# The gate's modulation columns: row pairs of the weight, four column quarters on separate array columns, the last pair at the 13th tile

## The chip, the cores and the metric

The kernel runs on one core of one Trainium2 chip. The metric is the time of one execution on the device, in microseconds (us). Before the change three runs took 1488.47, 1492.28 and 1495.5 us; the median is 1492.28 us.

## The reference, cut to what matters

One layer of a decoder trunk is computed for a prompt of 2048 rows and for 8 sample rows. Everything starts with a modulation made from a condition vector c, of which there are nine (one for the prompt, eight for the samples):

```python
mod = jnp.einsum("nd,de->ne", jax.nn.silu(c), w_ada) + b_ada      # d = 1024, e = 3 * 1024
shift, scale, gate = jnp.split(mod[:, None, :], 3, axis=-1)
h = _rmsnorm(x, norm_g) * (1.0 + scale) + shift
z = jnp.einsum("nld,de->nle", h, w_in)                             # 3840 columns: 30 tiles of 128
...                                                                # four branches, from z
return x + gate * jnp.einsum("nle,ed->nld", y, w_out)
```

shift and scale are needed ahead of everything else, because h needs them. gate, the last 1024 columns of `mod`, is needed only at the end, when the output projection is scaled by it. The change is about how these 1024 gate columns are computed: nine rows, a sum over 1024, weights of 4 MB.

## The kernel before, in words

Each engine has its own instruction queue, written out by hand, and the queues meet by semaphores. The first stage normalizes x and turns it, and multiplies the shift and scale columns (`mod_chunk`, L899). Then h is split into a high and a low part (`h_hi`, `h_lo`).

The second stage is the input projection: 30 tiles of 128 output columns. `project` (L968) multiplies one tile over five groups of up to 416 rows (banks 0 to 4 of PSUM), for each group 8 steps of the sum by three matmuls (`three`, L934: high by high, high by low, low by high). Meanwhile ScalarE and VectorE split the weights of the next tile (`split_w`) and empty the banks (`evac`), SyncE stores the tile (`store`), and GpSimd's queue loads the weights of the tile after next (`load`). All four follow the same order of tiles (`walk`, L374), numbered t from 0, so that tile 12 is the 13th.

The gate columns stand between tile 1 and tile 2 of this stage. Their weight is cut by columns: four quarters of 256 columns, each with all 8 steps of the sum, 1 MB each, in two buffers `gate_w` (L166). SyncE loads quarters 0 and 1 ahead of the projection (L640 to L644), when the first stage has left the places of the buffers (the squares' scratch `junk` and the modulation's bias `b_mod`). TensorE multiplies a quarter in `gate_columns` (L939): 8 matmuls of 9 by 256 columns into partitions 0 to 8 of bank 5. VectorE adds the bias of the quarter into `mod_gate` (L1533 to L1537) and so frees bank 5 for the next quarter. SyncE loads quarters 2 and 3 into the two buffers as soon as quarters 0 and 1 are multiplied (L684 to L688); in its queue this stands behind the store of tile 1.

From tile 12 on, eight chunks of the pooling and convolution branch run beside the projection. Their rows are loaded back by GpSimd's queue (`chunk_load`, L827) into places that lie over the gate weights' buffers, VectorE works on them (`chunk`, L1447), and TensorE multiplies two small matrices in bank 5 (`pool_matmul`, L949), from tile 13 on, behind the third group of rows.

`mod_gate` is read for the first time at the start of the output stage (L1134). The attention in between (from about 806 us to 1226 us) works on units of 128 queries; its `weigh_values` (L1054) is of interest for one thing: it writes head 0 to partitions 0 to 63 and head 1 to partitions 64 to 127 of the same bank, from matmuls of 64 output columns each (L1067). `decode` has matmuls of 48 columns at partition 0 (L1109) and of 32 columns at partition 64 (L1112).

Of the kernel before, what the change touches and what calls it, by code (L numbers as in the profile page):

```python
# [19 lines left out]
P = 128  # L20
D = 1024
KD = D // P
T = 2048
NS = 8
# [51 lines left out]
def build_program(nc, x_prompt, x_sample, c_t, w_ada, b_ada, norm_g, w_tiles, const, pool_w, pool_scale,  # L76
# [4 lines left out]
    with ExitStack() as ctx:  # L81
# [16 lines left out]
        def sem(name):  # L98
            return ctx.enter_context(nc.semaphore(name))
# [20 lines left out]
        mod_gate = keep.put("mod_gate", [NS + 1, D])  # L120
# [4 lines left out]
        c_silu = keep.put("c_silu", [P, KD, NS + 1])  # L125
# [10 lines left out]
        b_gate = keep.put("b_gate", [NS + 1, D])  # L136
# [6 lines left out]
        slot_at = w_at + 6 * D * 4  # L143
        SLOT = TT * 4
# [18 lines left out]
        junk = Plan(slot_at + 2 * SLOT).put("junk", [P, D])  # L163
        b_mod = Plan(slot_at + 3 * SLOT).put("b_mod", [NS + 1, 2 * D])
        mod_sb = Plan(slot_at + 4 * SLOT).put("mod_sb", [NS + 1, 2 * D])
        gate_w = [Plan(slot_at + (2 + b) * SLOT).put(f"gate_w{b}", [P, KD, 256]) for b in range(2)]  # L166

        cp = Plan(slot_at + 2 * SLOT)
        u_in = cp.put("u_in", [P, 2, HALO + CH])
# [82 lines left out]
        psum = ctx.enter_context(nc.psum_tensor("psum", [P, 8, 512], F32))  # L252
# [4 lines left out]
        x_loaded = [sem(f"x_loaded{i}") for i in range(4)]  # L257
        xs_loaded = sem("xs_loaded")
        ada_loaded = sem("ada_loaded")
        gate_loaded = [sem(f"gate_loaded{i}") for i in range(2)]  # L260
        c_ready = sem("c_ready")
        sumsq = sem("sumsq")
        rstd_ready = sem("rstd_ready")
# [7 lines left out]
        mod_t = sem("mod_t")  # L271
# [12 lines left out]
        gate_mm = sem("gate_mm")  # L284
        gate_added = sem("gate_added")
# [318 lines left out]
        wv = w_ada.rearrange("(k p) e -> p k e", p=P)  # L604
# [6 lines left out]
        def _(sp):  # L611
# [28 lines left out]
            sp.wait_ge(sumsq, 17)  # L640
            sp.wait_ge(mod_added, 4)
            sp.wait_ge(mod_mm, 4)
            for q in range(2):
                sp.dma_start(gate_w[q][:], wv[:, :, 2 * D + 256 * q:2 * D + 256 * q + 256]).then_inc(gate_loaded[q], 16)  # L644

            def nat_store(n, g, t):

# [14 lines left out]
            def store(t, half, ts, kind):  # L662
                b = ts % 2
                one = lambda a, i: a[bass.ds(i, 1), :, :].rearrange("a p t -> p (a t)")
                for n, g in turns(ts - 1) if ts >= 12 else ():
                    nat_store(n, g, ts - 1)
                sp.wait_ge(bank_free[4], t + 1)
                if V0 <= ts < K0:
                    pass
                elif kind == "plain":  # L670
                    sp.dma_start(one(plain_dram, t), main[b][:, 0:T]).then_inc(main_stored[b], 16)
                elif kind == "gate":
                    sp.dma_start(one(gate_dram, t - GATE0), main[b][:, 0:T]).then_inc(main_stored[b], 16)
                else:
                    sp.dma_start(qk_dram[t - K0, 0].rearrange("h r t -> (h r) t"), main_hi[b][:, 0:T].bitcast(F32)).then_inc(
                        main_stored[b], 16)
                    sp.dma_start(qk_dram[t - K0, 1].rearrange("h r t -> (h r) t"), main_lo[b][:, 0:T].bitcast(F32)).then_inc(
                        lo_stored[b], 16)
                if 0 <= ts - CHUNK0 < NCH:
                    n = ts - CHUNK0  # L680
                    sp.wait_ge(yac_ready, n + 1)
                    sp.dma_start(yac_dram[:, :, CH * n:CH * n + CH].rearrange("m p t -> p m t"), yac[:]).then_inc(
                        yac_stored, 16)
                if ts == 1:  # L684
                    for q in range(2):
                        sp.wait_ge(gate_mm, q + 1)
                        sp.dma_start(gate_w[q][:], wv[:, :, 2 * D + 512 + 256 * q:2 * D + 768 + 256 * q]).then_inc(
                            gate_loaded[q], 16)  # L688

            walk(sp, store)  # L690

# [116 lines left out]
        def _(pool):  # L808
# [18 lines left out]
            def chunk_load(n):  # L827
                c0 = CH * n
                if n == 0:
                    for b in range(2):  # L830
                        pool.wait_ge(main_stored[b], 16 * 6)
                else:
                    pool.wait_ge(yac_ready, n)
                h = HALO if n else 0
                h2 = 2 if n else 0
                def rows(a, c, left, dst):
                    pool.dma_start(dst, a[:, :, c - left:c + CH].rearrange("m p t -> p m t")).then_inc(chunk_loaded, 16)
                rows(plain_dram[0:2], c0, h, u_in[:, :, HALO - h:])
                rows(plain_dram[2:4], c0, h2, ch_in[:, :, 2 - h2:])
                rows(plain_dram[4:6], c0, h2, cc_in[:, :, 2 - h2:])  # L840
                rows(plain_dram[6:8], c0, 0, cb_in[:])
                rows(gate_dram[0:4], c0, 0, gate_in[:])
# [45 lines left out]
        def _(pe):  # L888
# [34 lines left out]
            for k in range(KD):  # L923
                m = pe.transpose(psum[:, 0, NS * k:NS * k + NS], x_in[0][0:NS, k * P:(k + 1) * P], ident[0:NS, 0:NS])
# [11 lines left out]
                pe.matmul(out, hi, mlo, start=False, stop=False)  # L936
                return pe.matmul(out, lo, mhi, start=False, stop=stop)  # L937

            def gate_columns(q):  # L939
                b = q % 2  # L940
                pe.wait_ge(gate_loaded[b], 16 * (q // 2 + 1))
                if q:
                    pe.wait_ge(gate_added, q)
                for k in range(KD):
                    m = pe.matmul(psum[0:NS + 1, 5, 0:256], c_silu[:, k, :], gate_w[b][:, k, :],
                                  start=(k == 0), stop=(k == KD - 1))
                m.then_inc(gate_mm, 1)

            def pool_matmul(n):  # L949
                pe.wait_ge(diff_ready, n + 1)  # L950
                for m in range(2):
                    mm = pe.matmul(psum[:, 5, CH * m:CH * m + CH], pool_w_sb[:, m, :], diff[:, m, :],
                                   start=True, stop=True)
                mm.then_inc(pool_mm, 1)
# [35 lines left out]

            project(0, 0, 0)
            project(1, 1, 1)
            for q in range(4):
                gate_columns(q)
            with pe.Fori(1, 6) as i:
                for b in range(2):
                    project(2 * i + b, b, 2)
            project(12, 0, 12)
            with pe.Fori(0, 2) as i:
                for b in range(2):  # L1000
# [132 lines left out]
            for n in range(2):  # L1133
                m = pe.matmul(bank(n), consts[0:NS + 1, C_SELP:C_SELP + P], mod_gate[:, 512 * n:512 * n + 512],  # L1134
                              start=True, stop=True)
# [242 lines left out]
        def _(dve):  # L1378
# [68 lines left out]
            def chunk(n):  # L1447
# [45 lines left out]
                                                    gate_in[:, m, :], ALU.mult, ALU.mult)  # L1493
                last.then_inc(yac_ready, 1)

            def evac(t, half, ts, kind):
                b = ts % 2
                if ts + 1 < NT:
                    split_w((t + 1, ts + 1))
                if kind == "plain" and ts >= 12:  # L1500
                    main_free(dve, ts)
                elif kind == "plain" and ts >= 2:
                    dve.wait_ge(main_stored[b], 16 * half)
                if ts == K0:
                    dve.wait_ge(yac_stored, 16 * NCH)
                if ts >= K0 + 2:
                    dve.wait_ge(lo_stored[b], 16 * ((ts - K0) // 2))
                if K0 < ts < Q0:
                    dve.wait_ge(kv_t, turns(ts - 1)[-1][0] + 1)
                for g, (c0, c1) in enumerate(GROUPS):  # L1510
                    n = min(c1, T) - c0
                    if kind == "plain":
                        dve.wait_ge(group_done, 5 * t + g + 1)
                        last = dve.tensor_copy(main[b][:, c0:c0 + n], bank(g, n))  # L1514
                    elif kind == "gate":
                        if g < 4:
                            continue
                        dve.wait_ge(act_evac, t - GATE0 + 1)
                    else:
                        dve.wait_ge(act_evac, V0 - GATE0 + 5 * (ts - K0) + g + 1)  # L1520
                        last = dve.scalar_tensor_tensor(main_lo[b][:, c0:c0 + n], bank(g, n),  # L1521
                                                        -0.125 if kind == "q" else 1.0,
                                                        main_hi[b][:, c0:c0 + n].bitcast(F32), ALU.mult, ALU.subtract)
                        if kind == "k":
                            last = dve.tensor_copy(k_nat[:, c0:c0 + n], bank(g, n))
                    if g == 4:
                        dve.tensor_copy(zs_t[:, bass.ds(t, 1), :].rearrange("p a s -> p (a s)"),
                                        psum[:, g, n:n + NS]).then_inc(bank_free[g], 1)
                    else:
                        last.then_inc(bank_free[g], 1)  # L1530
                if 0 <= ts - CHUNK0 < NCH:
                    chunk(ts - CHUNK0)
                if ts == 1:  # L1533
                    for q in range(4):
                        dve.wait_ge(gate_mm, q + 1)
                        dve.tensor_tensor(mod_gate[:, 256 * q:256 * q + 256], psum[0:NS + 1, 5, 0:256],
                                          b_gate[:, 256 * q:256 * q + 256], ALU.add).then_inc(gate_added, 1)  # L1537

            walk(dve, evac)

# [412 lines left out]
```

## Time and profile before

| | |
|---|---|
| three runs | 1488.47, 1492.28, 1495.5 us |
| the profiled execution | 1488.72 us, its span from first to last instruction 1485.9 us |
| TensorE busy | 1369.2 us, 92% of the span |
| VectorE busy | 715.7 us, 48% |
| ScalarE busy | 463.3 us, 31% |
| GpSimd busy | 155.0 us, 10% |
| mean granted TensorE clock | 0.971 of full |

All times of a trace are us from the start of the span. The 2.8 us between the span and the time of the profiled execution lie outside the first and last instruction. A matmul on data of type fp32 leaves two records, each with a weight load of its own; one on fp32r leaves one. A record's duration runs from its start to the end of its result, so that records that follow closely overlap, and what one costs in a stream is the distance from start to start.

### The profile page before, as it was taken

The page shows a single profiled execution, that of the slowest core. Times are in us where ns is not written, and L with a number is a line of the kernel's source. Part 1 is how long each engine was busy: PE and PEld are TensorE (multiplying, and loading weights), DVE is VectorE, ACT ScalarE, POOL GpSimd, SP SyncE. Part 2 cuts the span into 40 slices and gives each one's busy share as a digit, 9 for nine tenths or more (in the row PEclk, how much of TensorE's full clock was granted, in tenths as well). Part 3 has the DMA queues.
Part 4 walks back from the last instruction along what each step waited for, and adds up shares of the span by engine and source line. Part 5 has one row for each costly group of instructions (what it writes and reads, how often), then busy time and mean ns, then how long its engine had stood idle before and what let it go on. Part 6 is the DMA issues. An engine that isn't in the chain of part 4 may idle for free.

```text
span 1485.9 us, 21646 instructions
## 1 busy us (share of the span) xinstructions
PE 1369.2 (92%) x7749; PEld 1189.7 (80%) x7749; DVE 715.7 (48%) x1835; ACT 463.3 (31%) x1190; POOL 155.0 (10%) x170
## 2 busy tenths in 40 slices
PE   5789999999999999999997799799979997999996
PEld 2376999999999998999996687678767765877774
DVE  3591111100344544232212557675777646788784
ACT  5530000121111101221111455565558541433431
POOL 0060000000122110000000012101110000111111
PEclk9989999999999999999999799989989998999998
DMA  9613121221353434434314995982594255454531
GB/s 322 225 54 110 57 85 42 85 85 42 114 199 119 152 114 142 136 107 172 116 69 143 234 231 139 250 175 62 127 234 137 94 171 177 154 177 159 172 124 47
DMA packets 125661, 206.31 MB, mean 139 GB/s; under 512 B 12835, under 2 KB 88260, under 8 KB 120045
## 3 DMA queue, kind: packets, MB, share of 16 engines
q1 hardware_dynamic: 112358, 160.12, 36.5%
q0 software_dynamic: 13216, 45.09, 9.3%
q8 instruction: 47, 0.77, 0.2%
q14 instruction: 40, 0.33, 0.1%
HBM read 136.34 MB, written 68.97 MB: 138 GB/s over the span
## 4 chain that ended last, share of the span: by engine, by line
PE 67%; issue 14%; DVE 5%; DMA 5%; SPq 4%; ACT 2%; POOL 2%; DVEq 0%; POOLq 0%; ACTq 0%
PE psum L935 15%; PE psum L936 15%; PE psum L937 15%; PE psum L1040 5%; PE psum L1067 4%; PE psum L1041 3%; PE psum L1051 3%; DMA v_dil<-dil_v_p 2%; SPq L423 2%; PE psum L906 2%; DMA dil_v_p<-kv_nat 2%; PE psum L1076 1%; POOL resid L882 1%; DVE h_f L1441 1%; PE psum L1109 1%
## 5 line engine op out<-in xcount | busy, mean ns | idle before, releaser
L935 PE MATMUL psum<-h_hi,w_hi 128*128 128x416 f32 (+1 forms) x1200 | 423.1, 353 | 12.6 <-POOL h_lo L814 12.6
L936 PE MATMUL psum<-h_lo,w_hi 128*128 128x416 f32 (+1 forms) x1200 | 420.9, 351 | 0.0
L937 PE MATMUL psum<-h_hi,w_lo 128*128 128x416 f32 (+1 forms) x1200 | 419.6, 350 | 0.0
L935 PEld LDWEIGHTS psum<-h_hi,w_hi 128*128 128x128 f32 x1200 | 226.6, 189 | 17.4 <-issue 14.6
L936 PEld LDWEIGHTS psum<-h_lo,w_hi 128*128 128x128 f32 x1200 | 226.8, 189 | 1.5
L937 PEld LDWEIGHTS psum<-h_hi,w_lo 128*128 128x128 f32 x1200 | 226.5, 189 | 1.3
L1308 ACT ACTIVATE probs<-logits,stats 128x256 f32<-128x256 f32 (+1 forms) x352 | 162.2, 462 | 166.9 <-DVE stats L1700 164.6
L1040 PE MATMUL psum<-k_both,q_both 128*128 128x256 f32 x352 | 149.0, 432 | 34.6 <-DMA v_dil<-dil_v_p 22.9
L1700 DVE CUSTOM_DVE_ANT_0 logits<-psum,bias_dil 128x256 f32<-128x256 f32 (+1 forms) x288 | 94.3, 363 | 98.9 <-PE psum L1041 78.6
L1040 PEld LDWEIGHTS psum<-k_both,q_both 128*128 128x128 f32 x352 | 93.6, 266 | 57.9 <-issue 31.9
L935 PE MATMUL psum<-wo_hi,y_hi 128*128 128x512 f32 x288 | 116.8, 405 | 10.9 <-DVE y_lo L1770 10.5
L1041 PE MATMUL psum<-k_both,q_both 128*128 128x256 f32 x352 | 124.0, 361 | 0.0
L936 PE MATMUL psum<-wo_lo,y_hi 128*128 128x512 f32 x288 | 113.7, 395 | 0.0
L937 PE MATMUL psum<-wo_hi,y_lo 128*128 128x512 f32 x288 | 113.7, 395 | 0.0
L1521 DVE SCALAR_TENSOR_TENSOR main_lo<-psum,main_hi 128x416 fp32r<-128x416 f32 (+1 forms) x45 | 26.3, 584 | 164.5 <-ACT main_hi L1270 164.5
L1514 DVE COPY main<-psum 128x416 f32<-128x416 f32 (+1 forms) x60 | 34.2, 583 | 143.5 <-PE psum L937 143.5
L1051 PE MATMUL psum<-consts,probs 128*128 128x128 f32 x574 | 96.7, 282 | 3.4 <-DVE probs_t L1688 3.4
L1222 ACT CAST w_hi<-w_raw 128x1024 fp32r<-128x1024 f32 x30 | 31.3, 1042 | 211.2 <-PE psum L937 189.1
L1041 PEld LDWEIGHTS psum<-k_both,q_both 128*128 128x128 f32 x352 | 96.0, 273 | 0.0
L1686 DVE COPY probs_t<-psum 128x512 f32<-128x512 f32 x111 | 76.7, 691 | 23.8 <-PE psum L1067 23.2
L1067 PE MATMUL psum<-probs_t,v_dil 128*64 128x128 f32 x900 | 82.3, 291 | 0.0
L1051 PEld LDWEIGHTS psum<-consts,probs 128*128 128x128 f32 x574 | 73.1, 146 | 9.3 <-issue 6.8
(244 smaller groups left out, 1558.6 us busy)
## 6 DMA issues: line engine op xcount, KB each, us to landing
w_raw<-w_tiles POOLq DMA_DIRECT2D x30, 512.0 KB, 5.7
k_both<-qk_dram SPq DMA_DIRECT2D x24, 512.0 KB, 13.9
mix_dram<-o_st POOLq DMA_DIRECT2D x36, 264.0 KB, 4.0
mix_in<-mix_dram SPq DMA_DIRECT2D x16, 594.0 KB, 4.0
gate_dram<-main SPq DMA_DIRECT2D x9, 1024.0 KB, 3.9
qk_dram<-main_hi SPq DMA_DIRECT2D x9, 1024.0 KB, 3.9
qk_dram<-main_lo SPq DMA_DIRECT2D x9, 1024.0 KB, 7.2
x_in<-x_prompt SPq DMA_DIRECT2D x16, 512.0 KB, 6.0
```

The lines of the kernel that those rows point to most:

```text
L935: pe.matmul(out, hi, mhi, start=start, stop=False)
L936: pe.matmul(out, hi, mlo, start=False, stop=False)
L937: return pe.matmul(out, lo, mhi, start=False, stop=stop)
L1040: pe.matmul(out, u.q(h), u.keys(0, h), start=True, stop=False)
L1041: m = pe.matmul(out, u.q(h), u.keys(1, h), start=False, stop=True)
L1051: m = pe.transpose(psum[:, PT_BANK + n % 2, P * k:P * k + P], probs[n % 4][:, h, c:c + P], ident)
L1067: m = pe.matmul(psum[64 * h:64 * h + 64, OT_BANK + g % 2, P * (n % 4):P * (n % 4) + P], u.v(h, back), probs_t[n % 2][:, k, :], start=(x == ...
L1222: nc.scalar.copy(w_hi[b][:], w_raw[b][:]).then_inc(w_hi_ready, 1)
L1308: m = nc.scalar.activation(probs[s % 4][:, h, u.cols()], xs_[s % 2][:, h, u.cols()], ACT.Exp, scale=-1.0, bias=st[:, s % 4, 2 * h:2 * h + ...
L1514: last = dve.tensor_copy(main[b][:, c0:c0 + n], bank(g, n))
L1686: dve.tensor_copy(dst[:], src).then_inc(pt_copied, 1)
L1700: m = dve.tensor_tensor_reduce(out=xs_[s % 2][:, h, c], in0=psum[:, S_BANK + s % 2, 256 * h + c.start:256 * h + c.stop], in1=u.bias(h), sc ...
```

## The change

The weight of the gate is cut by rows of the sum and not by columns. A load now brings two of the 8 steps, whole rows of 1024 columns, 1 MB as before. There are three buffers, so three of the four loads stand ahead of the projection; the third lies over `mod_sb`, and SyncE therefore waits also for the transposes that read it (`mod_t`). The fourth goes into buffer 0 when the first pair is multiplied, at the same place in SyncE's queue as before.

On TensorE `gate_rows(q)` takes the place of `gate_columns(q)`: for each of the pair's two steps, four matmuls of 9 by 256, quarter y into partitions 32 y to 32 y + 8 of bank 5. The four sums stay open in bank 5 over all four pairs. Pairs 0 to 2 stand where the four quarters stood, between tiles 1 and 2; pair 3 stands ahead of tile 12. VectorE's four bias additions move from behind tile 1 to the start of tile 12's `evac`, ahead of the split of tile 13's weights, with one semaphore at the start and one at the end.

Two waits are new on account of the shared places: the first `chunk_load` waits for the fourth pair's matmuls, and each `pool_matmul` for the additions.

```diff
-        gate_w = [Plan(slot_at + (2 + b) * SLOT).put(f"gate_w{b}", [P, KD, 256]) for b in range(2)]
+        gate_w = [Plan(slot_at + (2 + b) * SLOT).put(f"gate_w{b}", [P, 2, D]) for b in range(3)]
@@ SyncE
-            for q in range(2):
-                sp.dma_start(gate_w[q][:], wv[:, :, 2 * D + 256 * q:2 * D + 256 * q + 256]).then_inc(gate_loaded[q], 16)
+            sp.wait_ge(mod_t, 1)
+            for q in range(3):
+                sp.dma_start(gate_w[q][:], wv[:, 2 * q:2 * q + 2, 2 * D:3 * D]).then_inc(gate_loaded[q], 16)
                 if ts == 1:
-                    for q in range(2):
-                        sp.wait_ge(gate_mm, q + 1)
-                        sp.dma_start(gate_w[q][:], wv[:, :, 2 * D + 512 + 256 * q:2 * D + 768 + 256 * q]).then_inc(
-                            gate_loaded[q], 16)
+                    sp.wait_ge(gate_mm, 1)
+                    sp.dma_start(gate_w[0][:], wv[:, 6:8, 2 * D:3 * D]).then_inc(gate_loaded[0], 16)
@@ GpSimd, chunk_load
                 if n == 0:
+                    pool.wait_ge(gate_mm, 4)
@@ TensorE
-            def gate_columns(q):
-                b = q % 2
-                pe.wait_ge(gate_loaded[b], 16 * (q // 2 + 1))
-                if q:
-                    pe.wait_ge(gate_added, q)
-                for k in range(KD):
-                    m = pe.matmul(psum[0:NS + 1, 5, 0:256], c_silu[:, k, :], gate_w[b][:, k, :],
-                                  start=(k == 0), stop=(k == KD - 1))
+            def gate_rows(q):
+                pe.wait_ge(gate_loaded[q % 3], 16 * (q // 3 + 1))
+                for x in range(2):
+                    for y in range(4):
+                        k = 2 * q + x
+                        m = pe.matmul(psum[32 * y:32 * y + NS + 1, 5, 0:256], c_silu[:, k, :],
+                                      gate_w[q % 3][:, x, 256 * y:256 * y + 256], start=(k == 0), stop=(k == KD - 1))
                 m.then_inc(gate_mm, 1)
             def pool_matmul(n):
                 pe.wait_ge(diff_ready, n + 1)
+                pe.wait_ge(gate_added, 1)
@@
-            for q in range(4):
-                gate_columns(q)
+            for q in range(3):
+                gate_rows(q)
             with pe.Fori(1, 6) as i:
                 for b in range(2):
                     project(2 * i + b, b, 2)
+            gate_rows(3)
             project(12, 0, 12)
@@ VectorE
+            def gate_rows():
+                dve.wait_ge(gate_mm, 4)
+                for q in range(4):
+                    m = dve.tensor_tensor(mod_gate[:, 256 * q:256 * q + 256], psum[32 * q:32 * q + NS + 1, 5, 0:256],
+                                          b_gate[:, 256 * q:256 * q + 256], ALU.add)
+                m.then_inc(gate_added, 1)
             def evac(t, half, ts, kind):
+                if ts == 12:
+                    gate_rows()
                 if ts + 1 < NT:
                     split_w((t + 1, ts + 1))
@@ at the end of evac
-                if ts == 1:
-                    for q in range(4):
-                        dve.wait_ge(gate_mm, q + 1)
-                        dve.tensor_tensor(mod_gate[:, 256 * q:256 * q + 256], psum[0:NS + 1, 5, 0:256],
-                                          b_gate[:, 256 * q:256 * q + 256], ALU.add).then_inc(gate_added, 1)
```

## Rows read from the trace of the kernel before

**Rows 1.** The page: span, and busy us (share, instructions) of each engine.

```profile
span 1485.9 us, 21646 instructions
...
PE 1369.2 (92%) x7749; PEld 1189.7 (80%) x7749; DVE 715.7 (48%) x1835; ACT 463.3 (31%) x1190; POOL 155.0 (10%) x170
```

**Rows 2.** The chain that ended last, by line, of 100 to 420 us.

```profile
by line: PE psum L935 31.1%; PE psum L936 31.0%; PE psum L937 30.9%; PE psum L945 3.4%; DMA gate_w<-w_ada 1.6%; POOL h_lo L814 0.9%; DVE h_f L1441 0.8%; PE psum L952 0.3%; issue 0.1%; DVE mod_gate L1536 0.1%
```

**Rows 3.** Timeline around the gate columns: start, duration, engine, line, [idle before, releaser].

```profile
129.92 0.34 PE L937 MATMUL psum<-h_hi,w_lo 128*128 128x392 f32 x1
...
130.20 3.62 PE L945 MATMUL psum<-gate_w,c_silu 128*9 128x256 f32 x16
...
133.85 4.60 SPq L687 DMA_DIRECT2D gate_w<-w_ada  x2
...
134.41 3.61 PE L945 MATMUL psum<-gate_w,c_silu 128*9 128x256 f32 x16 [0.60 <-DVE mod_gate L1536]
...
139.13 3.62 PE L945 MATMUL psum<-gate_w,c_silu 128*9 128x256 f32 x16 [1.10 <-DMA gate_w<-w_ada]
...
143.34 3.61 PE L945 MATMUL psum<-gate_w,c_silu 128*9 128x256 f32 x16 [0.59 <-DMA gate_w<-w_ada]
...
146.89 0.46 PE L935 MATMUL psum<-h_hi,w_hi 128*128 128x416 f32 x1
...
146.99 0.41 DVE L1536 TENSOR_TENSOR mod_gate<-psum,b_gate 9x256 f32<-9x256 f32 x1 [3.80 <-PE psum L945]
147.18 0.35 PE L936 MATMUL psum<-h_lo,w_hi 128*128 128x416 f32 x1
```

**Rows 4.** Stretches: window, length, busy us by engine (instructions), clock, DMA share, GB/s.

```profile
130.10:146.90 16.80, 14.51 (x66) 5.54 (x65) 1.86 (x5) 1.04 (x1) 0.00 (x0) 1.00 0.55 187
146.90:384.70 237.80, 237.80 (x1273) 236.01 (x1273) 32.46 (x52) 26.60 (x36) 9.41 (x16) 1.00 0.20 74
```

**Rows 5.** The gate weights' tile: durations (ns, min/median/max), and landing of its loads.

```profile
L945 PEld LDWEIGHTS psum<-gate_w,c_silu x64: 87/91/91, 130.2 to 146.4; 128*9 128x9 f32 x64
L945 PE MATMUL psum<-gate_w,c_silu x64: 376/379/384, 130.2 to 146.6; 128*9 128x256 f32 x64
...
DMA to landing us min/median/max: 5.2/5.3/7.8
```

**Rows 6.** Timeline in the attention, a unit's two heads on two column halves (L1067).

```profile
881.11 0.42 PEld L1067 LDWEIGHTS psum<-probs_t,v_dil 128*64 128x64 f32 x8 [0.17 <-issue]
881.11 0.67 PE L1067 MATMUL psum<-probs_t,v_dil 128*64 128x128 f32 x8
```

**Rows 7.** Timeline of the next unit: full-width transposes of 128 columns (L1051).

```profile
882.84 0.62 PE L1051 MATMUL psum<-consts,probs 128*128 128x128 f32 x4
```

**Rows 8.** Line L1067: durations of its weight loads and matmuls (ns, min/median/max).

```profile
L1067 PEld LDWEIGHTS psum<-probs_t,v_dil x900: 132/136/232, 834.2 to 1223.8; 128*64 128x64 f32 x180
L1067 PE MATMUL psum<-probs_t,v_dil x900: 272/273/477, 834.2 to 1223.9; 128*64 128x128 f32 x180
```

**Rows 9.** Timeline in the attention: 48 columns at partition 0, then 32 at partition 64.

```profile
1180.67 0.81 PE L1109 MATMUL psum<-dec_v,dec_pz 128*48 128x384 f32 x2
...
1181.40 0.41 PE L1112 MATMUL psum<-dec_sv,dec_psz 128*32 128x128 f32 x2
```

**Rows 10.** Timeline at the end of the first stage: transposes of mod_sb, SyncE's gate loads.

```profile
67.56 1.15 PE L929 MATMUL psum<-consts,mod_sb 9*128 9x9 f32 x16 [0.17 <-DVE mod_sb L1407]
67.58 1.02 SPq L644 DMA_DIRECT2D gate_w<-w_ada  x2
```

**Rows 11.** Timeline at the start of tile 12, all engines.

```profile
371.25 0.35 PE L935 MATMUL psum<-h_hi,w_hi 128*128 128x416 f32 x1
...
372.90 1.23 DVE L1418 TENSOR_TENSOR w_lo<-w_raw,w_hi 128x1024 fp32r<-128x1024 f32 x1 [0.65 <-ACT w_hi L1222]
```

**Rows 12.** Timeline of GpSimd's queue: the first chunk's first load.

```profile
376.88 0.72 POOL L837 DMA_DIRECT2D u_in<-plain_dram  x1 [24.36 <-DMA gate_dram<-main]
```

**Rows 13.** A stretch with the clock at half for a part, columns as in rows 4.

```profile
820.00:850.00 30.00, 22.76 (x164) 18.90 (x166) 16.63 (x63) 14.87 (x55) 0.76 (x1) 0.79 1.11 229
```

More of the change, by code:

```diff
@@ L259, in build_program @@
         ada_loaded = sem("ada_loaded")
-        gate_loaded = [sem(f"gate_loaded{i}") for i in range(2)]
+        gate_loaded = [sem(f"gate_loaded{i}") for i in range(3)]
         c_ready = sem("c_ready")
```

## The prediction

> **What bounds the kernel now.** I read the page first: TensorE is busy for 92% of the span [rows 1], the next engine for 48%. A share over the whole span says little of one place, so the second view is the chain that ended last, from 100 to 420 us, which holds the gate columns and the tiles behind them. 93% of it is the projection's matmuls; 3.4% is the gate's matmuls (L945), 1.6% a gate weight's load, 0.1% the bias addition [rows 2]. So the gate columns lie whole on the path. The stretches say the same of what comes behind: from 146.9 to 384.7 us TensorE is busy for 237.80 of 237.80 us, at full clock [rows 4]. Whatever is saved ahead of it moves all of it forward.
>
> The third view is the timeline there [rows 3]. The reader is to see four blocks of 16 records, starting at 130.20, 134.41, 139.13 and 143.34 us, and the projection going on at 146.89. In a block the records start (3.62 - 0.38) / 15 = 0.216 us apart [rows 3, 5], so a block takes 16 x 0.216 = 3.46 us of TensorE. The distances of the blocks are 4.21, 4.72, 4.21 and 3.55, so between them lie 0.75, 1.26, 0.75 and 0.09 us. The first and third 0.75 are the round trip over VectorE's addition and its semaphore or the load that is just in time; the 1.26 is the wait for the load that SyncE issued only at 133.85, when the first block was done. The last projection record before starts at 129.92, the gate's first 0.28 later, of which 0.09 is the price of a change of shape (below, [rows 9]); so TensorE would go on at about 130.10 if there were no gate. **The price of the gate columns now is 146.89 - 130.10 = 16.8 us**: 13.8 of matmuls, 2.8 of waits, 0.1 at the entry and 0.1 at the exit.
>
> **Removed at tile 2.** All 2.8 us of waits: bank 5 isn't emptied between pairs, and no load is on the path. The loads' cover: SyncE now also waits for the transposes of mod_sb, which end at 68.7 us, instead of issuing at 67.58 [rows 10]. Two loads landed after at most 7.8 us [rows 5], so three take some 4 more, and the last lands by about 81 us. It is needed at 130, behind 49 us of projection; if that cover were gone, it would cost those 4 us. The same queue's next item is the store of tile 0, which has to be multiplied first. What else is late at 133 us? Tile 2's weights lie in tile 0's buffers, free while tile 1 runs; banks 0 to 3 are emptied while tile 1 runs; nothing in the chain [rows 2] stands between gate and projection but these loads and additions.
>
> **Multiplying three pairs.** These are 24 matmuls of the same shape as before, so 48 records. Whether they cost 48 x 0.216 or a quarter hangs on whether matmuls on separate array columns run side by side. The trace has no case with four. The nearest is the attention's L1067, with two heads on two halves of the columns: 8 records of 128 columns in 0.67 us [rows 6], each 0.27 long [rows 8], so (0.67 - 0.27) / 7 = 0.057 us from start to start. Full-width records of 128 columns, four in 0.62 us [rows 7], start (0.62 - 0.27) / 3 = 0.12 apart if each lasts as long. So two halves do run at the same time, at twice the rate. Four abreast would give rounds of 0.216 us: 48 / 4 x 0.216 = 2.6 us. One more bound stands beside it, how quickly records follow at all: 16 tiny transposes in 1.15 us, each 0.20 long, start 0.063 us apart [rows 10], and 48 x 0.063 = 3.0 us. L1067's 0.057 lies below that, so it isn't a hard floor. I take 2.8, and keep 2.6 and 3.0. A change between array shapes costs what rows 9 show: the second record of 48 columns starts about 0.32 after the first, at 1180.99, and the next shape follows 0.41 after that, so 0.09. Before, the gate already paid it at entry and exit. The projection then goes on at 130.20 + 2.8 + 0.1 = 133.1 instead of 146.89: **13.8 us less**.
>
> First weighing. The rows show eight weight loads of 0.136 us each [rows 8] done in 0.42 us [rows 6], so loads for two column halves overlap. The Trainium skill, "TensorE: Matmul & The Clock Gate", Part 3, says that a weight load overlaps matmuls in flight only where the row group differs; here all four quarters use all rows. Rows 6 speak against that rule. If it held nevertheless, four loads of 0.091 [rows 5] would make a round 0.364 us, 4.4 us for three pairs and 1.5 for the fourth, and the saving would be 2.1 us smaller. This is inside my range. The same section gives a measured speedup of 2.38 for three column tiles; by that, as an estimate, four would reach 3.2, and the saving is 1 us smaller.
>
> **Added at tile 12.** The fourth pair, 16 records: 16 x 0.058 = 0.93 us (0.86 to 1.0), and now an entry and an exit of its own that was not there: 0.09 in, 0.10 out, and 0.10 more on the first projection records (the second starts 0.29 after the first [rows 3] and not 237.80 / 1273 = 0.19 [rows 4]). That is **1.2 us more**, all on the path, since TensorE goes from tile 11 to tile 12 without a gap [rows 4]. Its weights were loaded 220 us earlier (SyncE's queue gets to that load after tile 1's store, about 131.5 us, and the next behind it is tile 2's store, a whole tile of (371.25 - 146.89) / 10 = 22.4 us later [rows 3, 11]).
>
> **Waits that are new.** (a) VectorE: four additions of 0.41 [rows 3] = 1.6 us ahead of the split of tile 13's weights. The wait for the fourth pair ends about 1 us after tile 11, when VectorE would be emptying tile 11's last bank and waiting for ScalarE's cast anyway; the split started at 372.90, 1.65 after tile 12 [rows 11], and would start perhaps 1 later. It is needed a tile's 22 us after tile 12 began. Behind it wait GpSimd's queue and TensorE's tile 13, both with that cover. Cost 0; without the cover 1 to 2 us. (b) GpSimd: the first chunk's load waits for the fourth pair, about 1.2 us after tile 11 ends; it waits anyway for tile 11's store, until 376.88, 5.6 us after tile 12 started [rows 11, 12]. Cost 0. Queued behind it are the chunk's other loads and the weights of tile 15. (c) TensorE: the wait for the additions ahead of each of eight pool products is long fulfilled. A fulfilled wait in the queue costs nothing at the tile borders, which have two each (no gap in 237.80 us, [rows 4]); a bound is 8 x 0.1 = 0.8 us if each cost a gap like an exit. I take 0. (d) The four additions vanish behind tile 1: VectorE's next work there is tile 3's split, not on the path.
>
> **Sum.** -13.8 + 1.2 = -12.6 us. Bounds of this case: -13.9 + 1.1 = -12.8, and -13.6 + 1.3 + 0.8 + 1 = -10.5. Against the profiled execution's own time, 1488.72: 1476.1. That execution lies 3.6 below the median of the three runs, 1492.28; the mean of all four times is 1491.2. The four spread over 7 us, and the clock explains how: the kernel has short stretches at half clock (1.2 GHz instead of 2.4), as in 820 to 850 us, where the mean is 0.79 [rows 13]: 30 x 0.21 / 0.5 = 12.6 us at half clock, worth up to 6 us. How many such stretches a run catches isn't in the change's hand. I put the sum against the mean: 1491.2 - 12.6 = **1478.6 us**.
>
> **Rivals.**
> 1. *Two abreast, not four* (10%). Rows 6 prove only two. Rounds pair up: 24 x 0.216 = 5.2 and 8 x 0.216 = 1.7 us, so the projection goes on at 135.5 and the fourth pair costs 2.0: -11.4 + 2.0 = -9.4, 1481.8 us.
> 2. *No overlap at all* (8%), the change doesn't do what it says: four quarters in one bank, or four streams of fp32, are taken in turn. Then 10.4 and 3.5 + 0.3 us; only the waits are saved: 13.8 + 2.8 of before against 10.4 + 3.8, so -2.4, 1488.8 us. For it: no row has four. Against it: L1067's halves share a bank too.
> 3. *Each turn drains the array* (2%), the one that makes it slower. If each record on another column group waits for the end of the one before, a record costs its whole 0.379 us [rows 5]: 64 x 0.379 = 24.3, with 0.5 for entries and exits 24.8 against 16.8: +8, 1499 us. It decides from a distance of (16.8 + 7.5 - 0.5) / 64 = 0.37 us per record. The Trainium skill, "TensorEngine Tiling (Array Packing)", Key Properties, says that a change of tiling mode drains the engine, a change of tile doesn't. Rows 9 price a change of shape at 0.09, and rows 6 show that a change of half within a shape has no such cost.
> 4. *Another half-clock stretch* (2%). The earlier, shorter gate moves every later stage against the clock's changes; one stretch more, priced as above, gives back 6 us: -6.6, 1484.6 us.
>
> **How the numbers follow.** Four abreast has 78%. Its times: 1488.47 - 12.8 = 1475.7 for the luckiest of before's runs, 1495.5 - 10.5 = 1485.0 for the other end. Below I add a little for a run luckier than those seen: 1473. Above, two abreast on a slow run gives 1495.5 - 9.4 = 1486, which is where the range ends; no overlap and draining, 10%, mostly lie beyond it. Range 1473 to 1486. Half a per cent, 7.5 us, is about what a measurement here can tell from no change; below 1484.8 is faster. Faster: nearly all of case 1's 78% and most of two abreast, 86%; same: no overlap and some of the rest, 11%; slower 3%.
>
> **What would show it.** Between tiles 1 and 2 one block of 48 records without a gap, first to last start about 2.7 us, the projection's first record at 133.1 (135.5 with two abreast, 140.9 with none); no addition on VectorE there; SyncE's loads from 68.7 and one at about 131.5. Ahead of tile 12, which starts at 371.25 - 13.8 + 1.2 = 358.7, 16 records in some 1.2 us, and four additions of 0.41 about 1 us into tile 12. The first chunk's load at about 376.88 - 13.8 = 363. The rest of the trace the same, 12.6 earlier. Wrong would be: a gap in the 48, records 0.1 or more apart, a weight load that starts after its matmul could, or a later stage that grows.

## The result, and the profile after

The changed kernel took 1469.01 us (median of four runs, 1465.73 to 1475.69); the kernel before 1490.67 us (four runs: the three shown above, and one more of 1489.07). The ratio is 0.9856, its 95% interval 0.9811 to 0.9901. That is 21.7 us less (15 to 28), where 12.6 less was forecast, and the time lies 4 us below the range. The profiled execution took 1475.69 us, the longest of the four, with a span of 1474.0; that is 13.0 less than the profiled execution of the kernel before.

The place that was changed first. The timeline of the changed kernel between tiles 1 and 2, which answers to rows 3 (start, duration, engine, line; PE is TensorE, PEld its weight loads, DVE VectorE, ACT ScalarE, POOL GpSimd, SPq SyncE's queue):

```profile
134.58 2.28 PEld L945 LDWEIGHTS psum<-gate_w,c_silu 128*9 128x9 f32 x48 [0.26 <-issue]
134.58 2.78 PE L945 MATMUL psum<-gate_w,c_silu 128*9 128x256 f32 x48
...
135.75 0.44 SPq L687 DMA_DIRECT2D gate_w<-w_ada  x1
135.77 1.23 DVE L1420 TENSOR_TENSOR w_lo<-w_raw,w_hi 128x1024 fp32r<-128x1024 f32 x1 [0.45 <-ACT w_hi L1224]
137.29 0.19 PEld L935 LDWEIGHTS psum<-h_hi,w_hi 128*128 128x128 f32 x1 [0.43 <-DVE w_lo L1420]
137.29 0.46 PE L935 MATMUL psum<-h_hi,w_hi 128*128 128x416 f32 x1
```

In place of four blocks there is one, 48 records without a gap. Following one another at 0.216 us as before they would take 10.4 us; they take 2.78. Two short stretches of the block (window, length, busy us and number of gate records in it, clock, DMA share, GB/s) show four records in flight from the first 0.03 us on, and no fifth for the next 0.19:

```profile
134.58:134.61 0.03, 0.03 (x4) 1.00 0.00 0
134.61:134.80 0.19, 0.19 (x4) 1.00 0.00 0
```

The projection goes on 137.29 - 134.58 = 2.71 us after the first gate record; before it was 16.69. The fourth load and the split of tile 3's weights come at once. And ahead of tile 12 (the same columns; for rows 11 and 12):

```profile
361.75 1.05 PE L945 MATMUL psum<-gate_w,c_silu 128*9 128x256 f32 x16
...
362.73 0.46 PE L935 MATMUL psum<-h_hi,w_hi 128*128 128x416 f32 x1
...
362.87 1.71 DVE L1501 TENSOR_TENSOR mod_gate<-psum,b_gate 9x256 f32<-9x256 f32 x4 [0.20 <-PE psum L945]
364.51 1.20 DVE L1420 TENSOR_TENSOR w_lo<-w_raw,w_hi 128x1024 fp32r<-128x1024 f32 x1
```
```profile
367.30 0.72 POOL L837 DMA_DIRECT2D u_in<-plain_dram  x1 [24.36 <-DMA gate_dram<-main]
```

The additions push the split of tile 13's weights to 1.78 us after tile 12's start (1.65 before), and the first chunk's load still waits for a store and not for the gate. The stretches of the changed kernel (window, length, busy us by engine, clock, DMA share, GB/s), for rows 4, show a full TensorE at full clock on both sides:

```profile
134.49:137.29 2.80, 2.80 (x49) 1.23 (x48) 1.86 (x3) 1.04 (x1) 0.00 (x0) 1.00 0.44 178
137.29:361.57 224.28, 224.28 (x1204) 222.52 (x1200) 29.50 (x48) 24.11 (x32) 5.29 (x10) 1.00 0.20 73
```

Then where the rest went. I took from both traces the time of the projection's first record in some of the tiles, and of the first one of the output projection (`wo_hi`):

| stretch, us | before | changed | difference |
|---|---|---|---|
| start to tile 0 | 75.9 | 80.3 | +4.4 |
| tile 0 | 31.8 | 31.8 | 0 |
| tile 1 and gate | 39.2 | 25.2 | -14.0 |
| tiles 2 to 11 (changed: and last pair) | 224.4 | 225.4 | +1.1 |
| tiles 12 to 20 | 221.7 | 217.1 | -4.6 |
| tile 21 to the output projection | 645.9 | 647.0 | +1.1 |
| output projection to the end | 247.1 | 247.2 | +0.1 |

So the change's own places give -14.0 and +1.2 (1.1, and 0.1 on tile 12's first records), as forecast. Two other stretches differ by as much as 5 us, in opposite directions, though nothing was changed in them. The first stage lost 4.4 us. Its TensorE stretch from 18 to 32 us, of the kernel before, of the changed one, and of its second trace (e1_again, below), columns as above:

```profile
18.00:32.00 14.00, 10.91 (x48) 4.83 (x48) 6.19 (x10) 6.67 (x13) 0.00 (x0) 1.00 0.94 354
```
```profile
18.00:32.00 14.00, 10.64 (x28) 3.26 (x27) 5.19 (x10) 5.54 (x13) 0.00 (x0) 0.76 0.95 358
```
```profile
18.00:32.00 14.00, 11.39 (x50) 4.86 (x48) 6.55 (x10) 7.36 (x14) 0.00 (x0) 1.00 0.94 348
```

The clock stood at half (1.2 GHz) for part of it, which falls on the first block of shift and scale columns: 16 records took 7.03 us before, 9.75 in the changed kernel, and 7.03 again in its second trace (timelines, in the same order). That is 2.7 of the 4.4 us; the other 1.65 is the block's later start, behind a wait for its weights' load:

```profile
21.85 7.03 PE L906 MATMUL psum<-ada_w,c_silu 128*9 128x512 f32 x16 [2.23 <-DMA ada_w<-w_ada]
```
```profile
23.50 9.75 PE L906 MATMUL psum<-ada_w,c_silu 128*9 128x512 f32 x16 [2.92 <-DMA ada_w<-w_ada]
```
```profile
21.55 7.03 PE L906 MATMUL psum<-ada_w,c_silu 128*9 128x512 f32 x16 [1.71 <-DMA ada_w<-w_ada]
```

The -4.6 lies in tile 20. There the transposes of tile 19 wait for ScalarE to copy the ones before, and that waits for a store to land. Before and changed kernel, ScalarE's and TensorE's timeline:

```profile
571.53 0.59 ACT L1249 COPY kv_nat<-psum 128x512 f32<-128x512 f32 x1 [2.91 <-DMA dil_v_p<-kv_nat]
...
568.68 0.66 PE L965 MATMUL psum<-consts,main 128*128 128x128 f32 x4 [0.78 <-ACT kv_nat L1249]
572.17 0.66 PE L965 MATMUL psum<-consts,main 128*128 128x128 f32 x4 [2.84 <-ACT kv_nat L1249]
```
```profile
558.58 1.03 PE L966 MATMUL psum<-consts,main 128*128 128x128 f32 x8
560.09 1.16 PE L966 MATMUL psum<-consts,main 128*128 128x128 f32 x8 [0.48 <-ACT kv_nat L1251]
```

In the first TensorE stands for 2.84 us and goes on at a mean clock of 0.57 for the next 3.7 us (stretch of the kernel before):

```profile
572.70:576.40 3.70, 3.70 (x15) 3.58 (x14) 1.55 (x4) 0.00 (x0) 0.00 (x0) 0.57 0.00 0
```

In the second neither happens. Whether this is the change's doing or chance was the question that the result left.

### The profile page after: what moved, and what is told of

Its sections match the earlier page's. It is cut to its first block, busy times and chain, and to the rows that moved or that the text cites. A ratio compares the mean times of both kernels' runs of the same rounds, so it can differ in the third digit from the quotient of the medians.

```text
span 1474.0 us, 21652 instructions
## 1 busy us (share of the span) xinstructions
PE 1359.2 (92%) x7749; PEld 1183.5 (80%) x7749; DVE 715.5 (49%) x1835; ACT 463.2 (31%) x1190; POOL 155.0 (11%) x170
## 4 chain that ended last, share of the span: by engine, by line
PE 67%; issue 14%; DVE 5%; DMA 5%; SPq 4%; ACT 2%; POOL 2%; POOLq 0%; DVEq 0%; ACTq 0%
PE psum L935 15%; PE psum L936 15%; PE psum L937 15%; PE psum L1042 5%; PE psum L1069 5%; PE psum L1043 3%; PE psum L1053 3%; DMA v_dil<-dil_v_p 2%; SPq L423 2%; PE psum L906 2%; DMA dil_v_p<-kv_nat 2%; PE psum L1078 1%; POOL resid L882 1%; DVE h_f L1443 1%; SPq L425 1%
```

## The experiments

**Theory A**: the change is worth the sum, about 12.8 us, and the other 9 us of the first comparison are chance, or belong to the occasion. **Theory B**: a later stage, that of tiles 12 to 20, runs shorter because it starts earlier, and the gain is really about 21 us. Two slips in the expectations: some call the stretch of 221.7 and 217 us "tile 12 to tile 20", and by the numbering used here it runs from tile 12's first record to tile 21's; and the first puts the 5 us in tiles 17 to 19, where they lie in tile 20.

**The changed kernel again** (e1_again; no edit).

> The changed kernel once more, unaltered. In the two profiles the gate's place gives back 14.0 us between tiles 1 and 2 and the pair ahead of tile 12 takes 1.2, net 12.8 us, as the sum had it; the four runs gave 21.7. Theory A (chance): the other 9 us are which waits and half-clock stretches fell into four runs on each side; a new series then gives about 12.8 us less than before, ratio 0.991 to 0.993. Theory B (a second effect): a later stage runs shorter because everything ahead of it is earlier; the ratio is again 0.984 to 0.987 (20 to 24 us), and the trace shows the stage of tiles 17 to 19 some 5 us shorter than before, as the first trace does.

Measured 1472.92 us beside 1485.69, ratio 0.9909 (0.9882 to 0.9937), that is 13.5 less. The means of 6 and 23 runs are 1473.1 and 1486.0: 12.9. Theory B's 0.984 to 0.987 lies outside the interval.

**The staging alone** (e2_unpacked): all on the same array columns, nothing side by side. VectorE adds the bias from banks 5 and 6 accordingly.

```diff
-                    for y in range(4):
+                    for y in range(2):
                         k = 2 * q + x
-                        m = pe.matmul(psum[32 * y:32 * y + NS + 1, 5, 0:256], c_silu[:, k, :],
-                                      gate_w[q % 3][:, x, 256 * y:256 * y + 256], ...)
+                        m = pe.matmul(psum[0:NS + 1, 5 + y, :], c_silu[:, k, :],
+                                      gate_w[q % 3][:, x, 512 * y:512 * y + 512], ...)
```

> The staging alone: row pairs, three loads ahead, the last pair ahead of tile 12, all as in the changed kernel, but each step of the sum is two matmuls of 512 columns into partitions 0 to 8 of banks 5 and 6, on the same array columns, so nothing runs side by side. Term by term: the waits of 2.8 us vanish, the matmuls cost 10.4 us at tile 2 and 3.5 + 0.3 at tile 12, net -2.4 us. Theory A: 1486 to 1490, ratio 0.998. Theory B: the later stage gives its 9 us here too, as it does not ask why it starts earlier: about 1480, ratio 0.992; if the 9 us hang on how much earlier it starts, something between.

Measured 1482.74, ratio 0.9983 (0.9962 to 1.0004), 2.5 us less: the staging without the packing is worth next to nothing. In the trace tile 1 and the gate take 32.9 us (39.2 before), tiles 2 to 11 with the last pair 228.0 (224.4), so the last pair gives back more than half of what the place between tiles 1 and 2 gained.

**The packing alone** (e3_pack_only): all four pairs between tiles 1 and 2, and VectorE's additions behind tile 1 again.

```diff
-            for q in range(3):
+            for q in range(4):
                 gate_rows(q)
...
-            gate_rows(3)
             project(12, 0, 12)
```

> The packing alone, at the old place: all four pairs between tiles 1 and 2, on four column groups, the additions behind tile 1. The fourth pair's load can't start before the first pair is multiplied and tile 1's store issued (131.4 us), and takes 5.2, so TensorE waits from about 132.9 to 136.7 and goes on at 137.7 instead of 146.9: -9.2 us. Theory A: ratio 0.994, about 1482. Theory B: 9 us more, 1473, ratio 0.988. In both the trace shows a wait of 3 to 4 us for the load ahead of the fourth pair; moving that pair to tile 12 is then worth 3.6 us of the change.

Measured 1481.64, ratio 0.9963 (0.9944 to 0.9982), 5.5 us less and not 9.2. Its timeline and three stretches say why:

```profile
129.87 2.78 PE L945 MATMUL psum<-gate_w,c_silu 128*9 128x256 f32 x48
...
131.04 0.43 SPq L687 DMA_DIRECT2D gate_w<-w_ada  x1
138.12 0.13 PEld L945 LDWEIGHTS psum<-gate_w,c_silu 128*9 128x9 f32 x8 [5.97 <-DMA gate_w<-w_ada]
138.13 1.90 PE L945 MATMUL psum<-gate_w,c_silu 128*9 128x256 f32 x16 [5.47 <-DMA gate_w<-w_ada]
```
```profile
132.60:138.10 5.50, 0.05 (x4) 0.00 (x0) 0.00 (x0) 0.00 (x0) 0.00 (x0) 0.90 0.87 289
138.10:147.00 8.90, 8.87 (x44) 7.29 (x45) 3.27 (x6) 0.00 (x0) 0.53 (x1) 0.68 0.19 58
```

The load landed 7.0 us after its issue, not 5.2. It follows the store of tile 1 after 0.4 us, and the DMA share is 0.87. In the changed kernel's three traces it does so too and lands after 7.1; in e2_unpacked, where it starts 2.9 us after the store, it takes 5.9, and in e7_no_gate (below), with no other transfer under way, 5.0. So the longer time goes with the transfers beside it and not with the load's cut by rows. And after TensorE had stood for 5.5 us its clock was 0.68 in the next 8.9 us; in it 16 records take 1.90 us where they take 1.05 in the changed kernel. By the first records, -6.6 us at the gate and +1.7 in the tiles behind, -4.9 in all. So the two halves of the change aren't a sum of two gains: staging alone -2.5, packing alone -5.5, together -12.9. Moving the last pair to tile 12 keeps TensorE from standing for a load that can't start earlier.

**Two column groups** (e5_two_wide) and **the loops exchanged** (e6_same_group), one run each (in e5_two_wide VectorE adds two halves of 512 columns):

```diff
# e5_two_wide
-                    for y in range(4):
+                    for y in range(2):
-                        m = pe.matmul(psum[32 * y:32 * y + NS + 1, 5, 0:256], ..., gate_w[q % 3][:, x, 256 * y:256 * y + 256], ...)
+                        m = pe.matmul(psum[32 * y:32 * y + NS + 1, 5, :], ..., gate_w[q % 3][:, x, 512 * y:512 * y + 512], ...)
# e6_same_group
-                for x in range(2):
-                    for y in range(4):
+                for y in range(4):
+                    for x in range(2):
```

> The changed kernel with two column groups in place of four: each step of the sum is two matmuls of 512 columns, into partitions 0 and 32 of bank 5. If the time of a round is that of one stream, records come in twos, 0.43 us from round to round: 12 rounds for three pairs, 5.2 us in place of 2.6, and 1.7 in place of 0.87 at tile 12; the time 3.5 us above the changed kernel's, which a single look will hardly show but the trace will. If groups only overlap in weight loads or latency, the rounds are longer than 0.43.

> The changed kernel with the two loops of a pair exchanged: both steps of quarter 0, then both of quarter 1 and so on, so that of each four records in the program's order all are on one column group (and the next four on the next). If TensorE starts matmuls strictly in the order of the program, neighbours can overlap only where the group changes: a block of 16 records takes about 13 x 0.216 = 2.8 us in place of 0.87. If it looks ahead to free groups (the attention's halves, in the same order, came in pairs 13 ns apart), the block takes 0.87 as before.

The block of three pairs on one column group (e2_unpacked), on two (e5_two_wide) and on four with the loops exchanged (e6_same_group), from the timelines:

```profile
131.00 10.47 PE L945 MATMUL psum<-gate_w,c_silu 128*9 128x512 f32 x24
```
```profile
129.69 5.32 PE L945 MATMUL psum<-gate_w,c_silu 128*9 128x512 f32 x24
```
```profile
133.74 2.80 PE L945 MATMUL psum<-gate_w,c_silu 128*9 128x256 f32 x48
```

Beside the 2.78 of the changed kernel these are 1, 2 and 4 times the rate; less the last record's own time (0.59 and 0.38), 9.9, 4.7 and 2.4 us. The exchanged loops cost nothing: of each four neighbouring records in the program all are on one column group, and TensorE still fills all four groups. The first stretches of e6_same_group's block show four records in flight at once, and none behind them, though the first two matmuls of the program (four records) are both on group 0:

```profile
133.73:133.78 0.05, 0.04 (x4) 1.00 0.00 0
133.78:133.95 0.17, 0.17 (x4) 1.00 0.00 0
```

The records don't name their group; that the four are on different ones follows from their starting 13 ns apart, where records on the same columns start 0.216 us apart. Here the Trainium skill, "TensorE: Matmul & The Clock Gate", Part 3, says that matmuls start strictly in the order of the program. The trace doesn't agree. In strict order three of each four records would wait 0.216 us for the one before, which makes 12 x 3 x 0.216 = 7.8 us, and with the last record's own 0.38 over 8; the trace has 2.80. e5_two_wide took 1477.49 us and e6_same_group 1477.47, single runs that decide nothing below their spread; by first records, two groups cost 2.6 + 0.8 = 3.4 us more than four, where 3.5 was expected.

**The kernel before again** (b1_before_again; no edit) and **with its gate twice** (b2_gate_twice):

```diff
-                for k in range(KD):
+                for k in list(range(KD)) * 2:
                     m = pe.matmul(psum[0:NS + 1, 5, 0:256], c_silu[:, k, :], gate_w[b][:, k, :],
```

> The kernel before, unaltered, for a second trace of it. The first trace's stage from the first record of tile 12 to that of tile 20 took 221.8 us; the changed kernel's two traces and the three variants' all have 217.0, give or take 0.2. Theory A (chance): it is a store that landed late in that one execution; a second trace of the kernel before shows about 217 too, and the time ratio is 1 within 0.3%. Theory B (before's own later stage is slower): 221 to 222 again.

> The kernel before with the cost of the gate's matmuls doubled: each quarter's 8 matmuls are done twice (the second pass starts the sum afresh). Four blocks of 3.46 us more on the path: +13.8 us less what the wider blocks hide of the waits for loads (the 0.5 us between round trip and late load in the third block). Ratio 1.009, 1499 where before has 1485.7. Theory A: everything behind only shifts, tile 12 to tile 20 takes about 217 us. Theory B (stages behind react to when they start): the total differs from +13.8 by several us, against the sign of the shift, so +18 to +23.

b1_before_again: 1484.36 beside 1486.41, ratio 0.9991 (0.9973 to 1.0009), and the stretch from tile 12 to tile 21 took 216.9 us. **That is the number that theory B needed to be 221 or more.** b2_gate_twice: 1501.60, ratio 1.0103 (1.0072 to 1.0135), 15.3 us more (11 to 20), where 13.8 less some 0.5 was due. Its trace has 52.5 us for tile 1 and gate, 13.3 above before, and 218.6 from tile 12 to 21. The price of the gate's matmuls is what the records say, and it is on the path one to one.

**The pairs in tile 0** (e4_in_tile0, e8_in_tile0_again), **without the gate's matmuls** (e7_no_gate), and **the changed kernel a third time** (e9_change_third). In tile 0 TensorE waits ahead of the steps of the sum for h_lo; the pairs go into those waits, and VectorE's additions stand behind tile 1. e7_no_gate is this version without the 32 gate matmuls: its loads, waits and semaphores stay, and `mod_gate` is the bias alone.

```diff
                     for k in range(KD):
+                        if k >= 4:
+                            gate_rows(k - 4)
                         pe.wait_ge(h_ready, k + 1)
...
-            for q in range(3):
-                gate_rows(q)
...
-            gate_rows(3)
             project(12, 0, 12)
# SyncE, ahead of its walk over the tiles
+            sp.wait_ge(gate_mm, 1)
+            sp.dma_start(gate_w[0][:], wv[:, 6:8, 2 * D:3 * D]).then_inc(gate_loaded[0], 16)
```

> A version that should beat both: the four pairs stand in tile 0, one ahead of each of the steps 4 to 7 of its sum, where TensorE waits for h anyway (7685 other records stay as they are; the trace shows 12.6 us of waits for h_lo there). The fourth load is issued behind the first pair, at about 88 us, and lands by 95. The whole 16.8 us of before are gone and nothing is added: theory A -16.8 us, ratio 0.989, 1474.5; theory B 9 us more, ratio 0.983, 1466. If the pairs don't fit into the waits, tile 0 ends up to 4 x 1.2 us later than at 130.1 and the gain shrinks by that.

> The floor: the kernel with the pairs in tile 0, but without the gate's matmuls (left out: the 32 matmuls of the gate columns; mod_gate is the bias alone). Its loads, waits and additions' places stay. If the pairs in tile 0 are wholly covered by the waits for h, this takes what that kernel takes, within 0.2% (about 1470, ratio 0.989); if they cost something there, it is faster by that.

> The kernel with the pairs in tile 0 once more, beside the changed kernel on one chip. By the landmarks of the traces it should be 2.9 + 1.2 = 4.1 us faster than the changed kernel: ratio 0.9887 against 0.9915.

> The changed kernel a third time. Theory A (the sum, -12.8 us): ratio 0.9915, between 0.989 and 0.994. Theory B (about -21 us in the mean): 0.986. The second series, on another chip, had 0.9909, and the stage that theory B names was 217 us long in a second trace of the kernel before too, so I expect theory A.

e4_in_tile0: 1470.36, ratio 0.9891 (0.9863 to 0.9918). e8_in_tile0_again: 1469.43, ratio 0.9858 (0.9835 to 0.9882). e7_no_gate: 1469.78, 0.9872 (0.9848 to 0.9897). e9_change_third: 1476.51, 0.9901 (0.9872 to 0.9930); its means are 1476.0 and 1488.9, again 12.9 apart. A pair in tile 0, from the timeline of e8_in_tile0_again:

```profile
98.08 0.34 PE L936 MATMUL psum<-h_hi,w_lo 128*128 128x392 f32 x1
98.35 1.05 PE L944 MATMUL psum<-gate_w,c_silu 128*9 128x256 f32 x16
99.51 0.43 PE L934 MATMUL psum<-h_hi,w_hi 128*128 128x416 f32 x1
```

From the last record of a step to the first of the next it is 1.43 us here, and 1.42 in the changed kernel's second trace, where nothing stands between them. Tile 0 takes 31.8 us in all of these traces, with the pairs and without. So in this place the gate is free: the version takes what the kernel without gate matmuls takes (1469.4 and 1469.8 on one chip). Against the kernel before it was expected at ratio 0.9887; the first series has 0.9891, the second 0.9858, with 0.9887 just outside its interval, and that series' gain of some 20 us is more than the 16.9 that the first records account for. Beside the changed kernel on one chip it is 7.1 us faster by the medians (1469.4 against 1476.5) and 2.6 on the other; the traces say 4. It is the version to keep.

## Why the prediction was right or wrong

The forecast time was wrong and the working of the sum was right. Point by point:

- **The price of the gate before, 16.8 us:** right. Without it at this place (e4_in_tile0) tile 1 takes 22.4 us in place of 39.2.
- **Multiplying three pairs, 2.8 us (2.6 to 3.0):** right, and the upper bound wasn't needed. From first record to projection 2.71 us; the records keep the round of one stream. The gain at this place was 14.0, forecast 13.8. Two abreast and no overlap, which together had 18%, are out; so is the drain. The first weighing went against the rule of the Trainium skill ("TensorE: Matmul & The Clock Gate", Part 3), as rows 6 had it: 48 weight loads of 0.091 us, 4.4 in turn, took 2.28. One figure of that paragraph was added up wrongly: with its speedup of 3.2, 10.4 and 3.5 us become 3.2 and 1.1, which is 0.6 us more than the sum has, and not 1.
- **Tile 12, 1.2 us:** right, 1.2. The waits called free were free: the additions began 0.14 us after tile 12 had begun and not about 1, the split moved by 0.13 and not by 1, and GpSimd's load waits for the same store as before.
- **The loads' cover:** right. They were issued from 73.19 us in this trace, 4.5 later than said since the first stage was longer, the last landed 9.2 us after its issue, at 83.3, and they were needed at 134.58.
- **From the sum to a time and a range:** this step failed. The prediction put the sum against 1491.2 us, the mean of four times of the kernel before, and its lower end on 1488.47, "the luckiest of before's runs". Neither bears that. In the three later series the kernel before has 63 runs: their mean is 1486.2, the lowest is 1479.81, and 49 of the 63 took less than 1488.47. With the lowest of them the same sum gives 1467, so the lower end of 1473 was some 6 us too high. The same kernels have, from series to series, medians of 1490.7, 1485.7, 1486.4, 1484.4 and 1489.7 (before) and 1469.0, 1472.9 and 1476.5 (changed): 1476.5 lies in the range, 1472.9 just below it, 1469.0 clearly below. Of the changed kernel's 16 runs 9 took less than 1473.
- **The change of 12.6 us:** right in the first records of the traces and in two further series, on two chips, which gave 12.9 in the means both times. The first comparison gave 21.7, with an interval (15 to 28) that leaves 12.6 out. Put against the means of the kernel before in the later series, 1484.6 to 1488.9, the sum would have given 1472.0 to 1476.3, where the changed kernel's later medians, 1472.9 and 1476.5, lie; the first one, 1469.0, is 3 us lower still.
- **The clock as the source of the spread:** the mechanism was right, its size too small. I allowed one stretch and 6 us in one place. The runs bear the clock out: of the 63 of the kernel before, the 28 with a mean clock of 0.971 or more took 1483.5 us on average, the 22 with 0.969 or less 1489.3, and the two groups' mean clocks, 0.9716 and 0.9683, are worth 0.0033 x 1486 = 4.9 of these 5.8 us. The thirteen traces, in stages that no edit touches, show three places: the projection starts at 74.8 to 80.3 us; tile 12 to 21 takes 216.8 to 217.2 in all but two, and 218.6 and 221.7 in those; from there to the output projection it varies by 6 us more. The first two vary within one kernel: 80.3, 75.7 and 80.0 in the changed kernel's three traces, and 221.7 and 216.9 in before's two. That it isn't the chip alone is shown for the first: on one chip, with a first stage that is the same, it is 75.4 in one trace and 79.5 in another (e5_two_wide, e6_same_group).

What stays open: why the first series alone came to 21.7. Its three quicker runs left no trace; their mean clocks were 0.971 to 0.973 and the slow one's 0.968, so the clock has a part in it. Three of before's four times were there before the changed kernel ran, and before's median differs by 5 us between series, so the two sides may not have been alike in chip; this was not tested. Theory B as stated has fallen.

## What to carry to other kernels

Matmuls with few output columns can stand side by side on the four groups of 32 array columns at nearly four times the rate, here with their four sums held open in one bank; that pays only where the weights are there, since a wait that the packing lays bare costs its length and the clock behind it. Look for the waits that TensorE has anyway and put the small work there: here 16.8 us of it went to nothing. And if the forecast change is the size of the spread between executions, make the range from the spread between series and not from one series' runs.

## What the runs showed of the hardware

- Four groups of array columns run independently for fp32 matmuls of 9 columns by 256: 24 matmuls in 2.78 us, on two groups (with 512 columns each, half as many) in 5.32, on one in 10.47.
- TensorE takes matmuls of free column groups ahead of earlier ones of busy groups: the order of the loops changes nothing (2.80 us against 2.78), and four records start within 0.04 us in either order.
- TensorE's clock fell after it had stood for 5.5 us (0.68 in the next 8.9) and after 2.84 us in one place; it did not after the waits of 0.6 to 1.1 us between the gate's blocks. In the first stage a stop of 2.81 us left it at full (e2_unpacked, 16 records in 7.03 us), and behind one of 1.93 it was at half for a part (b1_before_again, 8.72), so the length of one stop doesn't decide it.
- A load of 1 MB by rows, 0.4 us behind a store of 1 MB, landed after 7.0 to 7.1 us (five traces), after 5.9 where it started 2.9 us behind it (e2_unpacked), and after 5.0 with no other transfer under way (e7_no_gate).
